# Reading the stored activations of a feed-forward layer back in pairs of blocks

## The reference

```
def swiglu(x, w_in, w_out):
    g, u = jnp.split(x @ w_in, 2, axis=-1)
    return (jax.nn.silu(g) * u) @ w_out

u = modulate(rmsnorm(h, ffn1_norm[l]), sh1, sc1)
h = h + 0.5 * gt1[:, None, :] * swiglu(u, ffn1_w_in[l], ffn1_w_out[l])
m = token_mixer(...)
h = h + gt2[:, None, :] * m
u = modulate(rmsnorm(h, ffn2_norm[l]), sh3, sc3)
h = h + 0.5 * gt3[:, None, :] * swiglu(u, ffn2_w_in[l], ffn2_w_out[l])
return rmsnorm(h, final_norm)
```

## Time and profile before

| | us |
|---|---|
| median of three runs | 2249.34 |
| lowest and highest | 2249.01, 2250.98 |
| the profiled execution | 2247.95 |
| its span, first to last instruction | 2246.2 |
| TensorE busy | 2173.8 (97%) |
| GpSimd busy | 1289.1 (57%) |
| VectorE busy | 1270.0 (57%) |
| ScalarE busy | 813.2 (36%) |

### The profile page before, as it was taken

The page is one execution under the profiler, slowest core; times in us unless marked ns, Lnnn a source line. Parts: engine busy times, 40 slices in busy tenths (PEclk is TensorE's granted clock), DMA queues, the critical chain, the costliest instruction groups (busy, mean ns, idle before and its releaser), DMA issues.

```text
span 2246.2 us, 27974 instructions
## 1 busy us (share of the span) xinstructions
PE 2173.8 (97%) x10311; PEld 1755.1 (78%) x10311; DVE 1270.0 (57%) x1975; ACT 813.2 (36%) x1509; POOL 1289.1 (57%) x1036
## 2 busy tenths in 40 slices
PE   7999999999999999999999999999999999999998
PEld 4688888887887777778787788888678888887886
DVE  6956666567857327655666202243965444457855
ACT  5522323233445314355545201022522333343444
POOL 5777878778854432312212233336778888769851
PEclk9999999999999999999999999999999999999999
DMA  9054444567333310011101113111053333355333
GB/s 347 27 171 155 138 160 144 170 208 253 94 103 114 103 47 1 11 29 38 29 20 38 40 54 122 47 47 42 25 172 123 104 108 107 105 202 201 99 96 111
DMA packets 223369, 236.28 MB, mean 105 GB/s; under 512 B 9839, under 2 KB 154370, under 8 KB 222978
## 3 DMA queue, kind: packets, MB, share of 16 engines
q1 hardware_dynamic: 223234, 234.49, 32.7%
HBM read 185.69 MB, written 48.76 MB: 104 GB/s over the span
## 4 chain that ended last, share of the span: by engine, by line
PE 75%; DVE 9%; ACT 4%; DMA 4%; issue 3%; POOL 3%; SPq 1%; DVEq 0%; ACTq 0%; POOLq 0%
PE ps L2405 30%; PE ps L2462 14%; PE ps L2276 13%; PE ps L2359 12%; DMA x_raw<-hid_dram 1%; POOL w_lo L1003 1%; DVE x_op L1843 1%; DVE h L2070 1%; DMA ada_full<-in_w_ada 1%; PE ps L2547 1%; PE ps L2657 1%; ACT h L1501 1%; PE ps L2321 1%; DMA q<-in_ffn_w_out 1%; PE ps L2622 1%
## 5 line engine op out<-in xcount | busy, mean ns | idle before, releaser
L2405 PE MATMUL ps<-t,w_hi 128*128 128x512 f32 x1280 | 395.4, 390 | 1.1 <-POOL w_lo L1003 0.9
L2462 PE MATMUL ps<-x_op,w_hi 128*128 128x512 f32 x1232 | 381.4, 391 | 9.3 <-DVE x_op L1843 8.0
L1003 POOL TENSOR_TENSOR w_lo<-w_raw,w_hi 128x512 fp32r<-128x512 f32 x240 | 348.5, 1465 | 54.3 <-ACT w_hi L1257 54.1
L968 POOL TENSOR_SCALAR w_hi<-w_raw 128x1024 fp32r<-128x1024 f32 x55 | 57.8, 1050 | 470.3 <-PE ps L2276 294.5
L1257 ACT ACTIVATE w_hi<-w_raw 128x512 fp32r<-128x512 f32 x240 | 143.2, 625 | 424.3 <-DMA w_raw<-in_ffn_w_in 175.5
L2405 PEld LDWEIGHTS ps<-t,w_hi 128*128 128x128 f32 x1280 | 239.5, 188 | 52.4 <-POOL w_lo L1003 2.6
L2462 PEld LDWEIGHTS ps<-x_op,w_hi 128*128 128x128 f32 x1232 | 230.3, 188 | 62.1 <-POOL w_lo L1003 9.5
L1003 POOL TENSOR_TENSOR w_lo<-q,w_hi 128x512 fp32r<-128x512 f32 x132 | 194.5, 1479 | 110.2 <-ACT w_hi L1257 110.0
L2405 PE MATMUL ps<-t,w_lo 128*128 128x512 f32 x640 | 249.1, 389 | 0.0
L2462 PE MATMUL ps<-x_op,w_lo 128*128 128x512 f32 x616 | 239.8, 389 | 0.0
L1843 DVE TENSOR_TENSOR x_op<-x_raw,x_op 128x512 fp32r<-128x512 f32 x154 | 161.9, 1062 | 106.7 <-ACT x_op L1267 105.9
(11 more groups left out here) (302 smaller groups left out, 4266.0 us busy)
## 6 DMA issues: line engine op xcount, KB each, us to landing
w_raw<-in_ffn_w_in SPq DMA_DIRECT2D x88, 512.0 KB, 4.3
hid_dram<-hid_raw SPq DMA_DIRECT2D x154, 256.0 KB, 5.3
x_raw<-hid_dram SPq DMA_DIRECT2D x154, 256.0 KB, 2.7
ada_half<-in_w_ada SPq DMA_DIRECT2D x96, 256.0 KB, 3.3
w_raw<-in_w_in SPq DMA_DIRECT2D x41, 512.0 KB, 3.8
q<-in_ffn_w_out SPq DMA_DIRECT2D x6, 2816.0 KB, 15.2
ada_full<-in_w_ada SPq DMA_DIRECT2D x24, 512.0 KB, 11.0
x_tile<-in_x SPq DMA_DIRECT2D x8, 512.0 KB, 5.0
```

Source lines behind the costliest of these rows:

```text
L968: nc.gpsimd.tensor_scalar(w_hi[:, slot, :], w_raw[:, slot, :], 1.0, 0.0, ALU.mult, ALU.add).then_inc(w_high, 1)
L1003: nc.gpsimd.tensor_tensor(lo, src, hi.bitcast(F32), ALU.subtract).then_inc(hs_ready, 1)
L2405: mm = nc.tensor.matmul(ps[bank][:], w[i], x[:, k, :], start=(first and k == 0 and q == 0), stop=(k == 3 and q == 2), skip_group_check=True)
L2462: mm = nc.tensor.matmul(ps[down_bank(p) + m][:], w[:, tile(m)], x_op[:, n % 3, x, :], start=(p in (0, 1, 3) and k == 0 and q == 0), stop=( ...
```

## The change

Blocks are read back two at a time: one DMA of 512 KB for blocks n and n + 1, n even, and one of 256 KB for block 76, which stands alone. So 39 issues stand where 77 did, in each of the two output phases. `x_raw` keeps its four places, now two pairs; each pair has one semaphore in place of one for each block. Since a pair overwrites blocks n - 4 and n - 3, its wait is on block n - 3. Calls of `hidden_in` with an odd n return without doing anything, and one of them (n = 7) is removed. The wait for all stores (`hid_out`) moves from between blocks 10 and 11 to ahead of the pair 10 and 11. The sequence of the other loads is as it was.

```diff
         def x_loaded(f, n):
 
-            j = n % 4
-            per = (DOWN_STEPS - j + 3) // 4
-            return x_in[j], 32 + 16 * (f * per + n // 4 + 1)
+            pair = n // 2
+            per = (20, 19)[pair % 2]
+            return x_in[pair % 2], 32 + 16 * (f * per + pair // 2 + 1)
...
             def hidden_in(f, n):
 
+                if n % 2:
+                    return
+                count = min(2, DOWN_STEPS - n)
                 if n >= 4:
-                    sp.wait_ge(x_ready, f * DOWN_STEPS + n - 3)
-                sp.dma_start(x_raw[:, n % 4, :], hid_dram[n // PAIRS, n % PAIRS]).then_inc(x_in[n % 4], 16)
+                    sp.wait_ge(x_ready, f * DOWN_STEPS + n - 2)
+                blocks_ = hid_dram.rearrange("a b p s -> (a b) p s")[n:n + count]
+                sp.dma_start(x_raw[:, n % 4:n % 4 + count, :], blocks_.rearrange("n p s -> p n s")
+                             ).then_inc(x_in[n // 2 % 2], 16)
...
                 quarter_load(f, 3, q10[:], 1, 0, 0, PAIRS)
                 sp.wait_ge(hs_used, n + 7)
                 quarter_load(f, 2, q00[:, 10:11, :], 0, 0, 10, 11)
-                hidden_in(f, 7)
                 hidden_out(f, LAST)
                 hidden_in(f, 8)
                 quarter_load(f, 4, q01[:], 0, 1, 0, PAIRS)
-                for i in range(9, 11):
+                hidden_in(f, 9)
+                sp.wait_ge(hid_out, 16 * (f + 1) * DOWN_STEPS)
+                for i in range(10, 12):
                     hidden_in(f, i)
-                sp.wait_ge(hid_out, 16 * (f + 1) * DOWN_STEPS)
-                hidden_in(f, 11)
                 quarter_load(f, 5, q11[:], 1, 1, 0, PAIRS)
                 for i in range(12, DOWN_STEPS):
                     hidden_in(f, i)
```

## The result

The changed kernel takes 2270.4 us (median of 4 runs, 2267.44 to 2271.63), the kernel before 2249.59 us (4 runs, 2249.01 to 2250.98). The ratio is 1.0086, 95% interval 1.0074 to 1.0098: slower, as forecast, but by 20.8 us and not by 12.8. The profiled execution of the changed kernel took 2271.18 us (span 2269.5).

What follows compares the result with a forecast made beforehand. The prediction took the DMA queue to bound each output phase's head and TensorE the rest. A late `q10` costs 5.0 + 7.8 = 12.8 us, other terms 0: 2249.34 + 12.8 = 2262.1 us, range 2259.5 to 2265.5, with the clock's case 2257 to 2267.

Steps and rivals of the forecast that it cites:

- The heads are bound by the queue, the rest by TensorE: Output phases: steps 0 to 12 limited by the DMA queue, losing 5.5 and 4.2 us; steps 13 to 76 by TensorE.
- `q10` goes out behind the split of block 3: SyncE's order: pair 6 and 7 goes out at 506.37, `q10` 0.4 us later, where it went out at 496.29.
- How long the queue then needs: DMA queue: 3.3 us for the pair, 7.5 for `q10`, which lands 5.0 and 8.2 us late in the two phases.
- What follows from a late `q10`: Head of each phase: step 5 and block 12 come late, shifting step 13 by 5.0 and 7.8 us, 12.8 together.
- The clock: Rival: TensorE's stops before step 5 bring half-clock spells, forecast at 0; otherwise 1.7 to 3.4 us per phase; chance 14%.
- Fewer transfers: Rival: a leaner queue removes ScalarE's waits for block 12, so the heads lose 9.7 us, giving 2239.6; chance 4%.
- no cover appeared: Rival: slack between `q10` and step 5 covers the delay, so the time stays at 2249.3 us; chance 4%.
- no pair starved the steady state: Rival: pairs landing over 8 us after issue cost one microsecond per extra microsecond at 62 pairs, 2324 us; chance 2%.
- the 6.5 us at its low end: Second phase's loss if the queue takes the pair for nothing; with 4.4 us in the first phase, 10.9 us.
- the doubtful 0.8: Second phase: extra 0.8 us from `q10` to block 12 that might not recur; block 12 is 7.4 to 8.2 us late.
- The high end: Upper bound of 16 us: a 3.7 us pair or a microsecond's queue pause per phase, and a microsecond for the mixer.

Runs made afterwards that it cites:

- experiment 1: Changed kernel, all pairs kept, with the pair of blocks 6 and 7 issued behind the load of `q10`; 2252.09 us, ratio 1.0009.
- experiment 2: Kernel before, single blocks, with block 6 waiting for the split of block 3 instead of block 2; 2265.24 us, ratio 1.0069.
- experiment 7: Kernel before with block 6 held until block 3 is split, measured again beside the changed kernel; 2265.87 us, ratio 1.0069.
- experiment 5: Changed kernel with the last tile's five stores, and all SyncE issues behind them, held until `q10` has landed; 2268.71 us, ratio 1.0075.
- experiment 6: Changed kernel with ten unused matmuls of ones in TensorE's wait before step 5; 2266.54 us, ratio 1.0062; measured again, 2267.31 us, ratio 1.0076.
- experiment 3: Kernel before, single blocks up to block 11, pairs from block 12 to the end; 2252.1 us, ratio 1.0009.

## Why the prediction was right about the cause and wrong about the size

- *The heads are bound by the queue, the rest by TensorE*: right. The stretches of steps 13 to 76 are unchanged; all the loss is in the heads.
- *`q10` goes out behind the split of block 3*: right, and shown from both sides. Undo it with the pairs kept, and a ratio of 1.0009 is left (experiment 1); do it alone without pairs and 1.0069 appears (experiments 2, 7).
- *How long the queue then needs*: this is the step that failed, 3.3 us for the pair and 7.5 us for `q10`. It put the landing of `q10` 5.0 and 8.2 us late; it was 9.1 and 9.7 us late. Counted from the start of step 0, in us:

| term | phase 1: predicted, measured | phase 2: predicted, measured |
|---|---|---|
| pair issued | 5.65, 6.75 | 6.91, 6.90 |
| pair lands after its issue | 3.3, 4.14 | 3.3, 3.75 |
| `q10` lands behind the pair | 7.5, 9.56 | 7.5, 8.48 |
| `q10` landed | 16.4, 20.45 | 17.7, 19.14 |
| the same in the kernel before | 11.4 | 9.5 |

 The first term: I took the moment of block 3's split as fixed; in the changed kernel that split took 1.78 us instead of 0.82 beside GpSimd's work. This is no effect of the change. The second profile of the changed kernel has 0.88 us again, and in the second phase the kernel before had 1.78 too:
```profile
506.06 0.88 DVE L1847 TENSOR_TENSOR x_op<-x_raw,x_op 128x512 fp32r<-128x512 f32 x1 [0.83 <-ACT x_op L1271]
```
 There the pair was issued at 5.64 us, as predicted, and the other two terms alone missed: the pair landed 3.77 and 3.87 us behind its issue and `q10` 9.60 and 8.23 us behind the pair, at 19.0 us in both phases, 2.6 and 1.3 us later than forecast. The second: the row of 3.7 us for another 512 KB load, which I kept as the upper end, was nearer than my 3.3; in experiment 5 it was 3.72 and 3.76. The third is the largest. I took the 7.5 us that a quarter needs in a queue that is never empty. Here the queue ran empty for some 5 us before the pair, and the stores, the next pair and `q01` were issued while `q10` was still under way; the first store landed at 523.62, ahead of `q10` at 524.01. Experiment 5 shows the part of what stands behind `q10`, 1 us in each phase; without it `q10` took 7.43 us in the second phase, so the empty queue ahead of it cost nothing there. The throughput shows the slow stretch in time, three windows of 1 us of the changed kernel (columns as rows 2):
```profile
515.00:516.00 1.00, 1.00 (x6) 0.84 (x5) 0.00 (x0) 0.86 (x2) 0.00 (x0) 1.00 1.07 401
...
518.00:519.00 1.00, 0.00 (x0) 0.00 (x0) 0.00 (x0) 0.05 (x1) 0.00 (x0) 1.00 1.05 358
...
520.00:521.00 1.00, 0.00 (x0) 0.00 (x0) 0.00 (x0) 0.00 (x0) 0.00 (x0) 1.00 0.99 250
```
 The DMA engines are busy throughout and move 358 and then 250 GB/s in place of 401. With all behind `q10` held back (experiment 5) two microseconds near the end of its transfer still ran at 376:
```profile
515.00:517.00 2.00, 0.00 (x0) 0.00 (x0) 0.00 (x0) 0.58 (x1) 0.00 (x0) 0.99 1.01 376
```
 The other 1.1 us, in the first phase alone, stays open. In each profile of a late `q10` it was there: `q10` landed 9.6 to 10.0 us behind the pair against 8.2 to 8.5 in the second phase, 8.5 against 7.4 in experiment 5, and 9.0 and 8.8 against 8.3 and 8.2 with single blocks (experiments 2 and 7). In all seven of them, in the first phase and never in the second, one packet of an instruction fetch holds one of the sixteen DMA engines for about 1 us while `q10` is under way; in the changed kernel it is 1.6% of 16 engines in 4 us:
```profile
q8 instruction: 1, 0.02, 1.6%
```
 That is a coincidence in time and not a test: nothing here separates the packet from whatever else differs between the two phases.
- *What follows from a late `q10`*: right in form. Step 5 came 3.63 us behind the landing (3.66 predicted). Block 12 landed 22.8 and 22.9 us behind it, not 23.5 and 23.9. But step 13 came 6.74 and 6.60 us behind the start of block 12's high part, where I had shifted it at 5.99 and 5.73: a second term, 0.8 us a phase, that wasn't carried. Block 12's low part took 1.73 us there instead of 0.99 in the first phase, beside a sum on GpSimd (line 641, from 547.34 to 548.64):
```profile
547.46 1.73 DVE L1847 TENSOR_TENSOR x_op<-x_raw,x_op 128x512 fp32r<-128x512 f32 x1 [1.23 <-ACT x_op L1271]
```
 The two nearly cancel, and the heads grew by 9.05 and 9.12 us. From the landing of `q10` to step 13 it was 29.56 and 30.11 us in the kernel before, 29.53 and 29.55 in the changed one, 29.5 in both phases of experiment 2 (29.5 and 30.6 in experiment 7): the head moves with that landing.
- *The clock*: within each of the two stops the granted clock fell to 0.50, the 1.2 GHz level, and stayed there for 10.24 us, longer than the 3.4 us of rows 18; 6.4 us of the first spell fell into the stop itself. Step 5 took 4.63 us where it took 2.86 in experiment 6, and step 13 still waited for block 12. So the forecast's value of 0 held: experiment 6 took the spells of the stops away, and the time from `q10` to step 13 stayed in the first phase and was no shorter in the second (30.2 and 29.6 us). The rival's times, 2265.5 to 2269 us, cover one measured median, 2267.3, and come near the other, 2270.4, but that is coincidence, since its mechanism cost nothing.
- *Fewer transfers*: 76 fewer were on balance worth nothing that can be measured (experiments 1, 3). The Trainium skill's page "DMA: Bandwidth & Descriptors" (Rules for kernel authors) advises to coalesce many small transfers, and the fixed cost of about 2.0 us that the prediction took from it is given there for DMAs issued from GpSimd, while here SyncE issues them. Here a block follows the one ahead by 0.65 us, and the runs side with the rows; whether merging pays where each transfer stands alone, no run here shows.
- *The other rivals*: no cover appeared, since GpSimd had been waiting for `q10` already; no pair starved the steady state.
- *The whole*: the heads grew by 18.2 us and not 12.8 in the first profile of the changed kernel, by 16.6 in the second (48.54 and 48.52 us). The median over the first four runs, 2270.4, stood 3.1 us above the later median of the same kernel, 2267.3. Both lie above the forecast of 2262.1 us and above the end of the range, 2267. The range ended short of the clock case's own 2269, and the 6.5 us at its low end don't follow from the terms: a pair that costs nothing gives 7.6 us in the second phase, 6.8 with the doubtful 0.8 off. The high end allowed one pause of a microsecond a phase, and several terms of up to a microsecond pointed the same way: the pair, what stands behind `q10`, the low part of block 12, the open term in the first phase, and in some profiles the split. The 5.1 us by which the rest of the program was longer in the first profile than in that of the kernel before are no part of the mechanism.

## What to carry to other kernels

When several small loads become one, ask first what the merged load waits for and what is issued behind it on the same queue: the merged wait is the latest of its parts, and everything behind inherits it. Here a weight load of 2816 KB stood behind it and landed 9.1 and 9.7 us late, once in each of two phases, while the saved issues had cost nobody anything. A load's time read in a busy queue can be too short for the same load with other transfers issued right behind it: 7.5 us became 8.2 to 8.5 in the second phase and 9.6 to 10.0, in part unexplained, in the first.

## What I had not expected of the hardware

- A load was delayed by what was issued behind it, five stores and then two loads: by about 1 us on `q10` in each phase (9.56 and 8.48 us with them, 8.53 and 7.43 with them held back; one profile of the second kind).
- The same VectorE sum of two 128x512 operands took 0.69 us alone and up to 1.78 us beside GpSimd. Here is the split of block 3 in the changed kernel, the sum that follows it, and GpSimd at that time:
```profile
508.51 1.78 DVE L1847 TENSOR_TENSOR x_op<-x_raw,x_op 128x512 fp32r<-128x512 f32 x1
510.21 0.68 DVE L1823 TENSOR_TENSOR hid_raw<-hid_raw 128x512 f32<-128x512 f32 x1
```
```profile
506.69 3.04 POOL L1007 TENSOR_TENSOR w_lo<-q,w_hi 128x512 fp32r<-128x512 f32 x2 [0.36 <-ACT w_hi L1261]
```
 The second of GpSimd's two instructions runs from 507.99 to 509.73, and the split ends 0.55 us behind it, as if it had begun only then. In this profile all 62 low parts of blocks that took over 1 us began while a GpSimd instruction was at work. The Trainium skill's "SBUF — State Buffer" (Who interferes with whom) has such a lock between a VectorE instruction with two inputs in SBUF and a GpSimd one that reads SBUF; these rows agree. It makes the moment of a split, and so of a load that waits for it, uncertain by a microsecond: in the first phase of the changed kernel the split of block 3 took 1.78 us in one profile and 0.88 in the other.
- SyncE's issues took longer behind a large load that had long to go: 0.6 to 1.7 us for one store or load behind `q10` in the changed kernel, 13 to 6 us ahead of its landing, against 0.33 to 0.52 us for the same stores in the kernel before, issued in the last 4 us before `q10` landed.
